# One body for 32 half experts on TensorE, and expert weights in rows of 16384 bytes

## The reference, cut to what matters

```python
def expert_choice_ffn(h, w_router, w1, w3, w2):
    B, L, D = h.shape
    cap = EC_CAPACITY * L // N_EXPERTS
    aff = jax.nn.softmax((h @ w_router).astype(jnp.float32), axis=-1)
    gate, idx = lax.top_k(aff.transpose(0, 2, 1), cap)
    xs = jax.vmap(lambda hb, ib: hb[ib])(h, idx)
    a = jnp.einsum('becd,edf->becf', xs, w1)
    b = jnp.einsum('becd,edf->becf', xs, w3)
    y = jnp.einsum('becf,efd->becd', jax.nn.silu(a) * b, w2) * gate[..., None].astype(h.dtype)
    return jax.vmap(lambda yb, ib: jnp.zeros((L, D), yb.dtype).at[ib.reshape(-1)].add(yb.reshape(-1, D)))(y, idx)
```

## Time and profile before

| | us |
|---|---|
| median of three runs | 3301.26 |
| profiled execution, its own time | 3291.43 |
| its span | 3289.7 |
| TensorE matmuls busy | 2851.3 (87%) |
| VectorE busy | 867.7 (26%) |
| ScalarE busy | 492.3 (15%) |
| GpSimd busy | 238.1 (7%) |

### The profile page before, as it was taken

The page is one execution under the profiler, slowest core; times in us unless marked ns, Lnnn a source line. Parts: engine busy times, 40 slices in busy tenths (PEclk is TensorE's granted clock), DMA queues, the critical chain, the costliest instruction groups (busy, mean ns, idle before and its releaser), DMA issues.

```text
span 3289.7 us, 70042 instructions
## 1 busy us (share of the span) xinstructions
PE 2851.3 (87%) x32580; PEld 2092.8 (64%) x32580; DVE 867.7 (26%) x1443; ACT 492.3 (15%) x862; POOL 238.1 (7%) x254
## 2 busy tenths in 40 slices
PE   6999999999976887887579999999999678878874
PEld 3555676666646787877535456666666378777773
DVE  4953223231142000000159422223311400000003
ACT  2011023331020000000020110333200200000001
POOL 0330000000000000000004100000000000000000
PEclk9999999999988999999889999999999899999997
DMA  7222201102127999999762221121021289999994
GB/s 303 102 109 103 116 29 60 78 26 83 77 81 251 353 349 346 358 349 344 279 236 103 108 99 69 34 79 54 26 109 52 83 306 361 349 348 363 356 340 158
DMA packets 128912, 611.22 MB, mean 186 GB/s; under 512 B 6256, under 2 KB 6256, under 8 KB 119024
## 3 DMA queue, kind: packets, MB, share of 16 engines
q1 hardware_dynamic: 112464, 550.52, 44.1%
q0 software_dynamic: 7168, 24.12, 3.1%
q10 hardware_dynamic: 8992, 32.11, 2.6%
HBM read 576.84 MB, written 29.88 MB: 184 GB/s over the span
## 4 chain that ended last, share of the span: by engine, by line
PE 76%; issue 8%; DVE 8%; DMA 6%; ACT 1%; POOL 0%; POOLq 0%; SPq 0%; DVEq 0%; ACTq 0%
PE ps L281 65%; DVE region_b L1033 4%; DMA ring<-in_w_exp 3%; PE ps L524 2%; DMA ring<-in_w_mix 2%; PE ps L651 1%; PE ps L497 1%; PE ps L507 1%; PE ps L578 1%; PE ps L561 1%; DVE rstd L990 1%; DMA region_x<-ffn_rows 0%; DMA ffn_rows<-region_b,rstd 0%; DVE rstd L982 0%; PE ps L436 0%
## 5 line engine op out<-in xcount | busy, mean ns | idle before, releaser
L281 PE MATMUL ps<-region_r,ring 128*64 128x80 f32 x24192 | 927.6, 237 | 211.7 <-issue 200.3
L281 PEld LDWEIGHTS ps<-region_r,ring 128*64 128x64 f32 x24192 | 892.7, 140 | 248.8 <-issue 237.5
L281 PE MATMUL ps<-hT,ring 128*128 128x320 f32 (+2 forms) x3600 | 1019.2, 441 | 20.7 <-DVE region_b L1021 11.1
L281 PEld LDWEIGHTS ps<-hT,ring 128*128 128x128 f32 x3600 | 610.6, 192 | 380.3 <-issue 237.7
L281 PE MATMUL ps<-region_b,ring 128*128 128x320 f32 (+2 forms) x896 | 257.5, 439 | 3.6 <-DMA ring<-in_w_mix 3.6
L1033 DVE SCALAR_TENSOR_TENSOR region_b<-region_b,params 128x655 f32<-128x655 f32 x240 | 243.8, 1016 | 8.5
L1219 DVE TENSOR_TENSOR region_r<-ps,region_r 128x320 f32<-128x320 f32 x64 | 31.5, 492 | 741.4 <-PE ps L682 741.4
L281 PEld LDWEIGHTS ps<-region_b,ring 128*128 128x128 f32 x896 | 159.3, 191 | 75.8 <-issue 23.3
L954 ACT ACTIVATE region_r<-ps 128x320 f32<-128x320 f32 x64 | 28.0, 438 | 1067.1 <-PE ps L682 1067.1
L281 PE MATMUL ps<-region_x,ring 128*128 128x512 f32 (+1 forms) x480 | 137.7, 445 | 3.7 <-DVE region_x L1159 3.7
L1224 DVE COPY region_r<-ps 128x320 f32<-128x320 f32 x64 | 31.5, 492 | 364.8 <-PE ps L682 364.8
(11 more groups left out here) (193 smaller groups left out, 2009.8 us busy)
## 6 DMA issues: line engine op xcount, KB each, us to landing
ring<-in_w_exp SPq DMA_DIRECT2D x192, 2048.0 KB, 10.7
ring<-in_w_mix SPq DMA_DIRECT2D x68, 2048.0 KB, 11.4
x_store<-region_m ACTq DMA_DIRECT2D x2, 2560.0 KB, 12.1
ffn_rows<-region_r ACTq DMA_DIRECT2D x4, 1280.0 KB, 18.0
region_m<-x_store ACTq DMA_DIRECT2D x2, 2560.0 KB, 10.5
h_rows<-region_x ACTq DMA_DIRECT2D x10, 512.0 KB, 2.7
region_x<-ffn_rows ACTq DMA_DIRECT2D x4, 1280.0 KB, 9.4
rstd<-in_bias POOLq DMA_DIRECT2D x16, 192.0 KB, 2.7
```

The lines of the kernel that those rows point to most:

```text
L281: ins = pe.matmul(*args, **kw)
```

## The change

The body for TensorE is now half an expert (`expert_half`): one block of w1, the transposes of four 128-column pieces of the tokens to come, one block of w3, the transposes of four pieces of a result three halves back, and one block of w2 two halves back. The first three halves are written out, halves 3 to 31 are a loop with this one body, and the last two w2 blocks are written out. The weights are stored in this order (`w_first`, `w_exp`, `w_last`), and SP loops with three loads per turn. `PIECE` becomes 16384, the length of a partition's row.

Tokens are gathered in half rows of 2048 bytes, from `h_rows` seen as 1280 half rows, with 34 gathers per layer (`FETCHES`) in place of 16. Since a body has only one place for them, tokens of the next expert are parked in `xs_next` and copied to `xs` once the current expert is through. silu results go to two buffers `sil`; the first half of the product is copied into `act` later. Two DVE instructions per layer compute the half-row indices.

```diff
-EPAIRS = NE // 2
+HALVES = 2 * NE
-PIECE = 4096
+PIECE = 16384
+FIRST_BLOCKS, LOOP_BLOCKS, LAST_BLOCKS = 4, 3 * (HALVES - 2), 2
+FETCHES = HALVES + 2
...
-                with sp.Fori(0, EPAIRS) as q:
-                    for b in range(2 * EXP_BLOCKS):
-                        s = (MIX_BLOCKS + b) % SLOTS
-                        load(s, l * per_layer(s) + q * (2 * EXP_BLOCKS // SLOTS)
-                             + first_in_slot(MIX_BLOCKS + b),
-                             a["w_exp"][l, q, b], PIECE)
+                def expert_load(b, src, turns=0):
+                    s = (MIX_BLOCKS + b) % SLOTS
+                    load(s, l * per_layer(s) + turns + first_in_slot(MIX_BLOCKS + b), src, PIECE)
+
+                for b in range(FIRST_BLOCKS):
+                    expert_load(b, a["w_first"][l, b])
+                with sp.Fori(0, LOOP_BLOCKS // 3) as t:
+                    for b in range(3):
+                        expert_load(FIRST_BLOCKS + b, a["w_exp"][l, t, b], t)
+                for b in range(LAST_BLOCKS):
+                    expert_load(FIRST_BLOCKS + LOOP_BLOCKS + b, a["w_last"][l, b])
...
+                def expert_half(i, n, turns, second, y_before):
+
+                    pe.wait_ge(S["xs_ready"], i + 1 if type(i) is not int or i else 2)
+                    if type(i) is not int or i:
+                        pe.wait_ge(S["sil_ready"], i)
+                    expert_block(n, turns, a_ps, xs, "a_done")
+                    if type(i) is not int or i:
+                        pe.wait_ge(S["xs_parked"], i)
+                    turn_rows(i + 2, i + 3)
+                    if type(i) is not int or i:
+                        pe.wait_ge(S["b_used"], i)
+                    expert_block(n + 1, turns, b_ps, xs, "b_done")
+                    if y_before:
+                        turn_y(i - 3)
+                    if second:
+                        pe.wait_ge(S["act_ready"], i - 1)
+                        expert_block(n + 2, turns, y_ps, act, "y_done")
+
+                turn_rows(0, 2, 0)
+                turn_rows(1, 2, 1)
+                expert_half(0, 0, 0, False, False)
+                expert_half(1, 2, 0, False, False)
+                expert_half(2, FIRST_BLOCKS, 0, True, False)
+                with pe.Fori(3, HALVES) as i:
+                    expert_half(i, FIRST_BLOCKS, i - 2, True, True)
+                for b in range(LAST_BLOCKS):
+                    turn_y(HALVES - 3 + b)
+                    pe.wait_ge(S["act_ready"], HALVES)
+                    expert_block(FIRST_BLOCKS + LOOP_BLOCKS + b, 0, y_ps, act, "y_done")
+                turn_y(HALVES - 1)
...
+                for i in range(HALVES):
+                    e, half = divmod(i, 2)
+                    v.wait_ge(S["rows_turned"], i + 3)
+                    v.tensor_copy(xs_next[:, half * HC:(half + 1) * HC], PS[2][:, 0, 0:HC]).then_inc(S["xs_parked"], 1)
+                    v.wait_ge(S["b_done"], i + 1)
+                    v.wait_ge(S["sil_ready"], i + 1)
+                    if half == 0:
+                        v.tensor_tensor(sil[0], PS[0][:, 1, 0:HC], sil[0], ALU.mult).then_inc(S["b_used"], 1)
+                        if e:
+                            copy_y(i - 2)
+                        continue
                     if e < NE - 1:
-                        take_rows(e + 1)
...
+                        v.wait_ge(S["xs_parked"], i + 1)
+                        v.tensor_copy(flat(xs), xs_next).then_inc(S["xs_ready"], 2)
+                    if e:
+                        copy_y(i - 2)
+                    link(v.tensor_tensor(flat(act)[:, HC:2 * HC], PS[0][:, 1, 0:HC], sil[1], ALU.mult), "b_used")
+                    v.tensor_copy(flat(act)[:, 0:HC], sil[0]).then_inc(S["act_ready"], 2)
...
+                def fetch_rows(n):
+
+                    if n >= 2:
+                        g.wait_ge(S["rows_turned"], n if n > 2 else 1)
+                    at = n if n < HALVES else n - 2
+                    g.indirect_dma_start(out=xs_half[n if n < 2 else 0], out_offset=None, in_=a["h_rows"],
+                                         in_offset=bass.IndirectOffsetOnAxis(ap=slot_half[:, at:at + 1], axis=0))\
                         .then_inc(rows_in, 16)
...
+                for n in range(3):
+                    fetch_rows(n)
+                for i in range(HALVES):
+                    if i + 3 < FETCHES:
+                        fetch_rows(i + 3)
+                    if i >= 4 and i % 2 == 0:
+                        add_rows((i - 4) // 2)
+                for e in range(NE - 2, NE):
+                    add_rows(e)
```

More of the change, by code:

```diff
@@ L191, in step_kernel @@
         ffn_tok = h_tok
-        xs_tok = region_b[0:CAP, 0:D]
+        xs_half = [region_b[0:CAP, b * 512:(b + 1) * 512] for b in range(2)]
         y_tok = region_b[0:CAP, D:2 * D]
@@ L226, in step_kernel @@
             best_found best_turned slot_ready h2_turned h2_tok h2_stored
[L227 removed]
+            rows_turned xs_parked xs_ready a_done b_done b_used sil_ready act_ready
             y_done y_copied y_turned y_scaled ffn_in0 ffn_in1 ffn_turned ffn_added""".split()
@@ L654, in turn, with turn_rows, turn_y, expert_block @@
                     return ins
[L656 to L662, removed]
-                    last.then_inc(S["rows_turned"], 1)
[L665 to L672, removed]
+                def turn_rows(g, fetched, b=0):
+                    pe.wait_ge(rows_in, l * (16 * FETCHES) + fetched * 16)
+                    for k in range(4):
+                        last = (pe.transpose if k == 3 else turn)(
+                            PS[2][:, b, k * CAP:(k + 1) * CAP], xs_half[b][:, k * P:(k + 1) * P], ident[0:CAP, 0:CAP])
+                    last.then_inc(S["rows_turned"], 1)
+                def turn_y(j):
+                    pe.wait_ge(S["y_copied"], j + 1)
+                    pe.wait_ge(S["y_scaled"], j + 1)
+                    for k in range(4):
+                        last = (pe.transpose if k == 3 else turn)(
+                            yt_ps[0:CAP, k * P:(k + 1) * P], yT[:, k, :], ident)
                     last.then_inc(S["y_turned"], 1)
-                def expert_block(q, n, ps, moving, done):
-                    w = weights(l, MIX_BLOCKS + n, q * (2 * EXP_BLOCKS // SLOTS))
+                def expert_block(n, turns, ps, moving, done):
+                    w = weights(l, MIX_BLOCKS + n, turns)
                     for m in range(4):
@@ L687, in expert_block @@
                     read(MIX_BLOCKS + n)
[L689 to L710, removed]
@@ L939, in _, with scale_y @@
                     sc.wait_ge(S["h2_tok"], t + 1)
[L940 to L944, removed]
+                    sc.dma_start(a["h_tok"][t * P:(t + 1) * P, :], h_tok[:, t, :]).then_inc(S["h2_stored"], 16)
+                def scale_y(j):
+                    e, half = divmod(j, 2)
+                    sc.wait_ge(S["y_turned"], j + 1)
+                    if e and not half:
                         sc.wait_ge(rows_added, l * (16 * NE) + 16 * e)
-                    for half in range(2):
-                        sc.activation(y_tok[:, half * 512:(half + 1) * 512], PS[3][0:CAP, half, :], ACT.Copy,
-                                      scale=slot_gate[:, e:e + 1]).then_inc(S["y_scaled"], 1)
+                    sc.activation(y_tok[:, half * 512:(half + 1) * 512], PS[3][0:CAP, 0, :], ACT.Copy,
+                                  scale=slot_gate[:, e:e + 1]).then_inc(S["y_scaled"], 1)
                 sc.wait_ge(S["slot_ready"], 1)
[L951 to L958, removed]
+                sc.sem_inc(S["y_scaled"], 1)
+                for i in range(HALVES):
+                    sc.wait_ge(S["a_done"], i + 1)
+                    if i >= 2:
+                        sc.wait_ge(S["act_ready"], i // 2 * 2)
+                    sc.activation(sil[i % 2], PS[0][:, 0, 0:HC], ACT.Silu).then_inc(S["sil_ready"], 1)
+                    if i >= 3:
+                        scale_y(i - 3)
+                for j in range(HALVES - 3, HALVES):
+                    scale_y(j)
                 sc.wait_ge(S["h2_stored"], 16 * TT)
@@ L1204, in layer_body @@
                 link(v.tensor_copy(slot_gate, PS[3][0:CAP, 0, 0:NE]))
+                for half in range(2):
+                    link(v.tensor_scalar(slot_half.rearrange("p (e b) -> p e b", b=2)[:, :, half],
+                                         PS[3][0:CAP, 0, NE:2 * NE], 2.0, float(half), ALU.mult, ALU.add))
                 link(v.tensor_copy(slot_row[:, :], PS[3][0:CAP, 0, NE:2 * NE]), "slot_ready")
[L1207 to L1219, removed]
-                    if e < NE - 1:
-                        take_rows(e + 1)
[L1222 to L1225, removed]
+                flat = lambda t: t.rearrange("p k c -> p (k c)")
@@ L1226, in layer_body @@
+                for j in range(HALVES - 2, HALVES):
+                    copy_y(j)
                 for k in range(KC):
```

41 lines of the change are left out of this document (24 added, 17 removed).

## The result

| | before | after |
|---|---|---|
| median, us | 3298.93 (4 runs) | 3167.29 (4 runs) |
| all runs, us | 3290.47 to 3306.66 | 3155.28 to 3169.49 |
| profiled execution, us | 3291.43 | 3167.31 |
| ratio | | 0.9594 [0.956, 0.9628] |

The change makes the kernel 4.1% faster. I had forecast 2.5%, 3220 us; the direction and the mechanism held, the gain that I forecast was 53 us too small.

A forecast was written before the change was run, and what follows sets the result against it. PE with its instruction-fetch gaps was taken to bound the expert stages. Without them transfers would set the pace: 3291.4 - 85.6 + 7 = 3213 us, the median 0.3% above, written as 3220, range 3165 to 3305 us.

The forecast's parts named there:

- The bound before: Expert stages: PE with gaps waiting for its program, 97.5 us of 560, sets the pace at 6.36 us per block.
- The body stays: TensorE's loop: body of 766 instructions stays in its memory, jump taken as 0, PE needing 15.5 us per half.
- Rivals 1 and 3: TensorE's loop: fetch gaps remain; rival 1 adds jump cost, the other keeps the old pace, 3301 us, chance 0.08.
- rival 1: TensorE's loop jump: body fetched again each turn, up to 4.17 us per turn more, 3540 us, chance 0.16.
- The price of the transfers: Expert-stage weight loads: 399 GB/s for 371.6, 97% busy, so 5.90 us per block, 85.6 us gained over two layers.
- The sum: Whole kernel: 3291.4 - 85.6 + 7 = 3213 us profiled, median 0.3% above it, written as 3220 us.
- start and end: Expert stage's start and end: an extra gather, index instructions and a scale's wait cost 3.4 us per layer, 7 us together.
- Gathers: Expert-stage row gathers: 18 more per layer, landing bounded by 10.8 us, fit in the 17.7 us turn and cost nothing.
- rival 2: Expert-stage gathers come late behind longer weight packets, landing at 24 us: 6.4 us more per turn, 3685 us, chance 0.04.
- The cover of DVE, ACT and POOL: Expert stage: extra copies, silu's other buffers and more gathers on these engines are hidden beside other work and cost nothing.
- The range: Whole kernel's time: 3165 to 3305 us, leaving out rival 1 and rival 2, to hold 8 in 10.

The follow-up runs named there:

- before_thin: The kernel before, with each expert block loading only the first 1024 of its 4096 columns, matmuls reading old contents for the rest: 3039.82 us, ratio 0.9215.
- body2: The changed kernel with two half experts in TensorE's loop body, one half more written out and 14 turns of two: 3347.59 us, ratio 1.0148 against the kernel before.
- loop_4k: The changed kernel with PIECE = 4096 again, the loop kept: 3182.85 us, ratio 0.9656 against the kernel before.
- pad40: The changed kernel with 40 tiny matmul calls added at the end of the loop body: 3449.95 us.
- pad110: The changed kernel with 110 tiny matmul calls added at the end of the loop body: 4321.93 us.
- before_16k: The kernel before with PIECE = 16384, all experts written out for TensorE as before: 3301.58 us, ratio 1.0007.
- written_4k: The changed kernel with the 29 turns written out instead of looped and PIECE = 4096: 3302.14 us, ratio 1.0008 against the kernel before.

## Why the prediction was right and where it was wrong

- **The bound before.** Right as far as it went: PE, waiting for its program, held the pace. Not every fetch leaves a gap: there are 74 for 91 packets. Not seen: the gap itself needs the transfer stream. The two limits were one; before_thin takes away the traffic, the changed kernel the fetches, and both lose the gaps.
- **The body stays.** Right, though only SP's loop stood for it. Rivals 1 and 3 fell for this body, and body2 shows rival 1 at work in a body twice as long, at more than the 4.17 us per jump that I had as its price. How long a body may be, nothing in the rows before had measured; that this one fits is shown only by the runs. By the 2048 instructions of the Trainium skill ("Runtime: NRT & Kernel Launch", Instruction fetch mechanics) body2 would have stayed as well, and it was fetched.
- **The price of the transfers.** This is the step that failed: "371.6 GB/s, in packets of 4096 bytes", "I take 399", and "at the same 97% busy". Demand was put at 504 us for 88 blocks, 5.73 us per block, and 5.90 at 97%. Measured: 5.54 per block at 100%. Of the 0.36 us between them about half is the 97% and half the demand. The 97% was taken from a stretch in which PE set the pace, and it was no ceiling but what PE's gaps left (100% and 102% in the changed kernel and loop_4k). The 399 GB/s was taken from the mixers, and 406 is reached. The 371.6 GB/s, from the stretch again, was hardly a property of short pieces: they run at 392 with the loop, and long ones at 372 in pad40. The forecast put 34.3 us of a stretch of 88 blocks down to the pieces, some 72 us of the kernel by the same rule of 93 blocks in each layer. Their whole worth is 16 us of the kernel with the loop and nothing without it; the rest of the 131.9 us came with the loop, which let the transfers run without a pause.
- **The sum.** Counted over a whole stage of 96 blocks, a block took 6.29 us in the first layer and 6.22 in the second, and takes 5.56 and 5.57 now. The 6.36 that I started from rests on 88 loads issued in 560 us, where one load more or less moves it by 0.07. The two stages became 69.9 and 62.0 us shorter, against 42.8 less 3.4 us forecast for each. The written-out halves at the start still cost something: from 1014 to 1080 us q8 brings 10 packets and PE is idle for 9.8 us on "issue", a term that my sum didn't have. The 3.4 us that I had for start and end is not measured by itself.
- **Gathers.** 8.2 us to landing, under the bound of 10.8 that I took from the earlier trace rows; rival 2 fell. The cover of DVE, ACT and POOL held: none of them is waited for in the stretch shown.
- **The range.** 3165 to 3305 holds the time at its very edge. That it holds it is in part luck: its fast end stood 20 us under the forecast's own range, which nothing in the sum called for. The forecast's own 3185 to 3245 missed. It varied the rate (395 or 403 GB/s) and the busy share (96 or 99%), and neither reached what was measured, 406 GB/s and 100%.

## What to carry to other kernels

A fetch of TensorE's program goes over the same DMA engines as the weights. Where 256 instructions are only 4.9 us of work, the fetch was hidden while these engines were quiet, and not beside the full stream; in the mixers, where they are 30 us of work, it was hidden too. Where small matmuls run under a full weight stream, count the "instruction" packets, and make the loop body short enough to stay; a body somewhat too long was worse than no loop. And when one engine sets the pace, neither the busy share nor the rate of another is its limit: take its own price from a stretch in which it is the bound.

## What the runs showed of the hardware that was not expected

- A loop body of 1234 TensorE instructions stays (pad110). Of one of 1585 (body2) 4.5 packets are fetched per turn, and its jump leaves PE idle for 7.0 us with busy DMA engines.
- TensorE's program comes in packets of 256 instructions; beside the full stream a gap ends 1.0 to 1.6 us after the packet has ended (kernel before).
- The rate in a queue's busy time depends on who sets the pace: rows of 16384 bytes ran at 406 GB/s where transfers were the bound, 376 and 372 where PE was. The median packet is the same; 9% of long ones, most of them soon after the issue of a load, make the difference (before_16k and pad40 against the changed kernel).
- With the gaps the granted clock was 0.97 in the stretch of the earlier trace rows, without them 1.00. written_4k kept the gaps and the old time at 0.965 over its whole span, the same as the changed kernel's 0.966. And the 5.17 us per block that PE needed at 0.97 would still fit in the changed kernel's 5.54, so the clock isn't what the gain came from.
